# The opening of a gated block kernel: first loads, the split of x, and TensorE before its inputs

## The reference

```python
proj = rmsnorm(x, gla_norm) @ gla_w_in        # 2048 x 6160
q, k, v, r, g_low = split(proj)               # k is computed first
...                                           # gated linear attention, output product
h = h + squared_relu_mlp(rmsnorm(h))          # 2048 -> 8192 -> 2048
h = rmsnorm(h, final_norm)
...                                           # second block: stick-breaking attention beside
                                              # a recurrent unit, input and output products
```

## Time and profile before

| what | value |
|---|---|
| median of 3 runs | 1518.81 us (1517.96 to 1520.08) |
| span of the profiled execution, first to last instruction | 1514.3 us |
| TensorE busy in that span | 1497.6 us |
| mean granted TensorE clock in that span | 1.000 |

### The profile page before, as it was taken

How to read it: one execution, slowest core, us unless ns; L and a number is a source line. 1 busy time by engine, 2 the same in 40 slices (tenths; PEclk the granted TensorE clock), 3 DMA queues, 4 the chain that set the end, 5 groups by cost and what they waited for, 6 DMA issues and landing times. The chain is left out here.

```text
span 1514.3 us, 19184 instructions
## 1 busy us (share of the span) xinstructions
PE 1497.6 (99%) x6826; PEld 1237.1 (82%) x6826; DVE 843.5 (56%) x872; ACT 711.9 (47%) x856; POOL 30.8 (2%) x54
## 2 busy tenths in 40 slices
PE   7999999999999999999999999999999999999998
PEld 6788888888888888888888888888888888888886
DVE  5555545555555545555555554555566776565653
ACT  5544544445444433443344433444654664565532
POOL 3000000000000000000000000000000011000000
PEclk9999999999999999999999999999999999999999
DMA  8455565657666666666666666666556566545564
GB/s 267 137 167 154 145 202 176 187 176 240 192 183 182 192 192 194 185 182 188 194 189 184 189 190 191 189 190 185 182 180 181 154 194 191 166 144 167 181 193 140
DMA packets 144721, 277.03 MB, mean 183 GB/s; under 512 B 10800, under 2 KB 10912, under 8 KB 144512
## 3 DMA queue, kind: packets, MB, share of 16 engines
q1 hardware_dynamic: 143056, 271.75, 59.3%
q0 software_dynamic: 1040, 3.07, 0.6%
q10 hardware_dynamic: 544, 1.05, 0.2%
HBM read 273.74 MB, written 2.10 MB: 182 GB/s over the span
## 5 line engine op out<-in xcount | busy, mean ns | idle before, releaser
L1003 DVE TENSOR_TENSOR w_lo<-raw,w_hi 128x1024 fp32r<-128x1024 f32 x508 | 620.2, 1225 | 610.7 <-ACT w_hi L706 609.3
L706 ACT ACTIVATE w_hi<-raw 128x1024 fp32r<-128x1024 f32 x508 | 537.0, 1059 | 731.7 <-PE acc L420 710.5
L418 PE MATMUL acc<-w_hi,xa_hi 128*128 128x512 f32 x1276 | 506.3, 397 | 1.6 <-issue 1.4
L420 PE MATMUL acc<-w_hi,xa_lo 128*128 128x512 f32 x1276 | 497.3, 390 | 0.0
L419 PE MATMUL acc<-w_lo,xa_hi 128*128 128x512 f32 x1276 | 496.7, 389 | 0.0
L418 PE MATMUL acc<-w_hi,xb_hi 128*128 128x512 f32 x768 | 300.1, 391 | 1.5 <-DVE w_lo L1003 1.5
L420 PE MATMUL acc<-w_hi,xb_lo 128*128 128x512 f32 x768 | 299.0, 389 | 0.0
L419 PE MATMUL acc<-w_lo,xb_hi 128*128 128x512 f32 x768 | 298.8, 389 | 0.0
L418 PEld LDWEIGHTS acc<-w_hi,xa_hi 128*128 128x128 f32 x1276 | 239.7, 188 | 52.0 <-issue 3.2
L420 PEld LDWEIGHTS acc<-w_hi,xa_lo 128*128 128x128 f32 x1276 | 239.5, 188 | 50.7
L419 PEld LDWEIGHTS acc<-w_lo,xa_hi 128*128 128x128 f32 x1276 | 239.9, 188 | 49.4 <-issue 1.9
(11 more groups left out here) (198 smaller groups left out, 513.1 us busy)
## 6 DMA issues: line engine op xcount, KB each, us to landing
raw<-in_mlp_w_up SPq DMA_DIRECT2D x128, 512.0 KB, 3.7
raw<-in_mlp_w_down SPq DMA_DIRECT2D x128, 512.0 KB, 4.4
raw<-in_gla_w_in SPq DMA_DIRECT2D x96, 512.0 KB, 3.8
raw<-in_w_in SPq DMA_DIRECT2D x96, 512.0 KB, 3.7
raw<-in_gla_w_out SPq DMA_DIRECT2D x32, 512.0 KB, 4.5
raw<-in_w_out SPq DMA_DIRECT2D x32, 512.0 KB, 4.7
result<-stage SPq DMA_DIRECT2D x8, 256.0 KB, 3.3
h<-in_x ACTq DMA_DIRECT2D x2, 512.0 KB, 6.4
```

Source lines behind the costliest of these rows:

```text
L418: pe.matmul(o, xh[:, kt, xs], w_hi[:, n % RING, k, :], start=kt == 0, stop=False)
L420: last = pe.matmul(o, xl[:, kt, xs], w_hi[:, n % RING, k, :], start=False, stop=kt == KT - 1)
L706: act.activation(w_hi[:, n % RING, :, :], raw[:, n % RING, :, :], ACT.Copy)\
L1003: dve.tensor_tensor(w_lo[:, n % RING, :, :], raw[:, n % RING, :, :], w_hi[:, n % RING, :, :].bitcast(F32), ALU.subtract).then_inc(lo_ready, 1)
```

## The change

The first loads are cut and ordered anew. The order in SP's queue becomes: `gla_norm`, chunk 0 in two halves of 256 KB, chunk 1, x columns 512 to 1023, chunk 2, x columns 1024 to 1535, chunk 3, x columns 1536 to 2047, `wg_raw`, then chunks 4 to 7. ScalarE's queue loads x columns 0 to 255 and 256 to 511 (256 KB each, with a semaphore for each). ScalarE splits group 0 of x ahead of chunk 0, and chunk 0 in two halves, each with a signal; VectorE makes `xa_lo` of group 0 ahead of `w_lo` of chunk 0. TensorE starts the first two matmuls of chunk 0 when the first half is there. `turn_x(c + 2)` now follows chunk c for c from 0 to 5. Around the first turns TensorE does 16 transposes of `ident` by `ident` whose result nobody reads.

```diff
@@ SP
-            for c in range(RING):
+            for k, done in ((0, first_in), (1, raw_in[0])):
+                sp.dma_start(raw[:, 0, k, :], w_in_v[:, k, GH * GDK:GH * GDK + N]).then_inc(done, 16)
+            for c in range(1, CH):
                 load(c, 0, None, CH, w_in_v[:, CK * c:CK * c + CK, GH * GDK:GH * GDK + N])
-
-            for j in (2, 3):
-                sp.dma_start(h[:, :, j * N:(j + 1) * N], x_v[:, :, j * N:(j + 1) * N])\
-                    .then_inc(x_in[j], 16)
-            sp.dma_start(wg_raw, w_in_v[:, :, 2 * GH * GDK + 2 * D:]).then_inc(wg_in, 16)
-            for c in range(RING, CH):
-                load(c, 0, None, CH, w_in_v[:, CK * c:CK * c + CK, GH * GDK:GH * GDK + N])
+                if c <= 3:
+                    sp.dma_start(h[:, :, c * N:(c + 1) * N], x_v[:, :, c * N:(c + 1) * N])\
+                        .then_inc(x_in[c + 1], 16)
+                if c == 3:
+                    sp.dma_start(wg_raw, w_in_v[:, :, 2 * GH * GDK + 2 * D:]).then_inc(wg_in, 16)
@@ TensorE, multiply_first
-                pe.wait_ge(hi_ready, 1)
+                pe.wait_ge(first_hi, 1)
...
+                        if kt == 1 and ws is w_hi and xs is xa_hi:
+                            pe.wait_ge(hi_ready, 1)
@@ TensorE, turn_x
-                if g % 2 == 0:
-                    pe.wait_ge(x_in[g // 2], 16)
+                if g < 2 or g % 2 == 0:
+                    pe.wait_ge(x_in[g if g < 2 else g // 2 + 1], 16)
@@ TensorE, after
-                    if c == 0:
-                        turn_x(2)
-                        turn_x(3)
-                    if 1 <= c <= 4:
-                        turn_x(c + 3)
+                    if c <= 5:
+                        turn_x(c + 2)
@@ TensorE, start
+            def keep_running(n):
+
+                for _ in range(n):
+                    pe.transpose(aux[:, 0, 0:P], ident[:, :], ident[:, :])
+
             pe.wait_ge(pool_chain, 2)
+            keep_running(6)
             pe.wait_ge(norm_in, 16)
             pe.transpose(aux[:, 1, 0:KT], rows[0:KT, :], ident[0:KT, 0:KT]).then_inc(par_turned, 1)
+            keep_running(5)
             turn_x(0)
             turn_x(1)
+            keep_running(5)
@@ ScalarE, start
-                act.dma_start(h[:, :, j * N:(j + 1) * N], x_v[:, :, j * N:(j + 1) * N])\
+                act.dma_start(h[:, :, j * S:(j + 1) * S], x_v[:, :, j * S:(j + 1) * S])\
                     .then_inc(x_in[j], 16)
 
-            act.wait_ge(raw_in[0], 16)
-            act.activation(w_hi[:, 0, :, :], raw[:, 0, :, :], ACT.Copy).then_inc(hi_ready, 1)
             act.wait_ge(par_ready, 1)
             split_x(None, 0, xa_hi, 0, C_GLA, 1)
+            for k, arrived, done in ((0, first_in, first_hi), (1, raw_in[0], hi_ready)):
+                act.wait_ge(arrived, 16)
+                act.activation(w_hi[:, 0, k, :], raw[:, 0, k, :], ACT.Copy).then_inc(done, 1)
@@ VectorE, start
             for n in range(RING):
-                if n:
-                    rest_x(n % 2, xa_hi, xa_lo, 2 * n, C_GLA, n + 1)
+                rest_x(n % 2, xa_hi, xa_lo, 2 * n, C_GLA, n + 1)
...
-                if n == 0:
-                    rest_x(0, xa_hi, xa_lo, 0, C_GLA, 1)
```

More of the change, by code:

```diff
@@ L197, in gated_block_kernel @@
         par_in, par_turned, par_ready = sem("par_in"), sem("par_turned"), sem("par_ready")
-        x_in = [sem(f"x_in{i}") for i in range(4)]
+        x_in = [sem(f"x_in{i}") for i in range(5)]
+        first_in, first_hi = sem("first_in"), sem("first_hi")
         gain_in, up_in, wg_in = sem("gain_in"), sem("up_in"), sem("wg_in")
```

## The result

| | before | after |
|---|---|---|
| median of 21 runs each, side by side | 1517.28 us | 1520.11 us |
| lowest to highest | 1514.63 to 1520.08 | 1518.12 to 1522.78 |
| span of the profiled execution | 1514.3 us | 1518.2 us |

The ratio is 1.0017, with a 95% interval from 1.0011 to 1.0023. The kernel is some 2.8 us slower by the medians, 2.7 by the means. That is under the 0.2% that the prediction called a change that can be told, but 21 runs tell it from none. The point forecast was no change.

The account below looks back on a forecast made before the run. The loads were taken to bound the kernel up to 26.5 us, TensorE after. The 2.4 to 4.1 us won at chunk 0 were all given back: span 1514.2 plus 4.5 gives 1518.7 us, range 1517.0 to 1521.3.

Parts of the forecast that it names:

- what paces the opening: Up to 26.5 us the loads set the pace, chunk 4 hanging on chunk 5's landing at 23.25; TensorE itself after it.
- The chunk 0 win: TensorE starts chunk 0 at 7.7 us instead of 10.14 and ends it 2.4 to 4.1 us earlier.
- Clock lost in the wait: Rival: TensorE's clock falls in the wait before chunk 4, costing 2.4 us and up to a microsecond more; 1521.1 us; chance 0.2.
- the fast start: TensorE runs chunk 0 at full clock from the start, chunk 3 ending at about 21.3 us; given half.
- a wait over 3.5 us: Condition for the clock to fall before chunk 4, read from 3.5 us of idleness ahead of a fall at the span's end.
- The wait of 2.8 to 5.1 us: TensorE's forecast idle time right before chunk 4, where it waited 1.0 us before the change.
- the likeliest case: The point forecast: the chunk 0 win is all given back at chunk 4, time 1518.7 us; chance 0.6.
- The bytes ahead of chunk 5 stay the same, as do POOL's: Loads: as POOL's instructions are untouched, chunk 4 still lands at about 21.9 us and chunk 5 at 23.25.
- thin pieces: Rival: x rows of 1 KB slow the loads, chunk 5 lands up to 1.0 us later, 1519.2 to 1519.7; chance 0.1.
- the forecast's 26.4: Start of chunk 4 on TensorE once group 4's xa_lo is ready, instead of 26.9 us before.
- the forecast's 35.7: Start of the gate matmuls on TensorE, from 32.93 + 2.74 us.
- The rule on transposes: By the skill, transposes do not count as clock activity; then the idle turns are for nothing and the start is slow.

Follow-up runs that it names:

- e3: The 16 turns of ident alone added to the kernel before; 1517.96 us, ratio 0.9998.
- e4: The new order of turns alone (group c + 2 behind chunk c) put into the kernel before; 1517.58 us, ratio 0.9998.
- e12: Kernel after plus x split two chunks sooner, 128x7 matmuls cut, o_gain held, ScalarE's table loaded up front, 14 ident turns behind chunk 3; 1518.62 us, ratio 1.0012.
- e14: Kernel after plus x split two chunks sooner, 128x7 matmuls cut, o_gain held, ScalarE's table loaded up front, no added ident turns; 1515.14 us, ratio 0.9987.
- e2: Kernel after without its 16 turns of ident; 1518.18 us, ratio 1.0005 to the kernel before.
- e13: Kernel after with POOL's load of o_gain started early, right behind that of b_gate; 1518.63 us, ratio 1.0013 to the kernel before.
- e8: Only the new loads of SP and ScalarE, with their semaphores, put into the kernel before; 1518.42 us, ratio 1.0009.
- e9: Kernel after with POOL's load of o_gain held until w_lo of chunk 8 is written; 1517.18 us, ratio 1.0000 to the kernel before.
- e1: Kernel after with 36 more turns of ident filling TensorE's wait ahead of chunk 4; 1517.40 us, ratio 0.9999 to the kernel before.
- e10: Kernel after with the wait ahead of chunk 4 filled by 36 ident turns and the 128x7 matmuls cut in halves; 1516.03 us, ratio 0.9995.
- e5: Kernel after with groups 4 to 7 of x split two chunks sooner by ScalarE and VectorE; 1517.31 us, ratio 1.0000 to the kernel before.
- e7: Kernel before with the 32 matmuls of 128x7 cut in two halves, two chunks apart; 1515.94 us, ratio 0.9991.

## Why the prediction was wrong, point by point

*Right: what paces the opening.* The loads set the pace up to chunk 4, through `w_hi`, `w_lo` and `xa_lo` of group 4. The chunk 0 win was 3.0 us, inside 2.4 to 4.1, and all was given back: forecast and found. e3 and e4 (0.9998 each) confirm that the idle turns and the order of turns are worth nothing by themselves. Chunk 0 started at 8.56, not 7.7. TensorE had no wait there; it was still at its turns, because columns 256 to 511 of x landed at 6.7, where before all 512 were there at 5.5:

```profile
6.70 1.11 PE L450 MATMUL tp<-ident,h 128*128 128x128 f32 x4 [0.93 <-DMA h<-in_x]
```

ScalarE's table load (1.28 us) also moved, from 1.8 us, where ScalarE had nothing to do, to 5.86, behind its wait for the first turn (ScalarE's rows above). It is not what set the start: e12 and e14 load the table at 0.81 and start chunk 0 at 8.62 and 9.25. The miss was free, since TensorE had to wait ahead of chunk 4 anyway.

*Wrong: the weight and the condition of the rival "Clock lost in the wait".* This rival is what happened, at its price: forecast 2.4 us and up to one more, found 2.7 in the trace. It was given a chance of 0.2 by two steps. The first, that it needs the fast start and a wait over 3.5 us, rested on one fall at the end of the span. e2 (2.48 us) and e13 (2.90) speak against the length, e2 and e8 (3.63), both without turns of `ident`, against the need of a fast start. The wait of 2.8 to 5.1 us that the forecast itself wrote down lies where such falls were seen (2.48 to 5.14 us, with 3.05 in e9 as the exception). The second step was to leave the likeliest case at full clock with such a wait in it.

*Mis-sized: "The bytes ahead of chunk 5 stay the same, as do POOL's".* The bytes did, their order did not. The 1.5 us of later landing are the late `o_gain` (e9, e13). The step took an untouched instruction list for an untouched timeline. As all of the wait sits ahead of chunk 4, it goes one to one into the end: 27.90 against the forecast's 26.4.

*Right: thin pieces do not delay chunk 5.* The row 8.56 to 12.30 has 386 GB/s, and e13 and e8, which have the same pieces, get chunk 5 at 23.29 and 23.36. The second piece of x itself did come late, at 6.7, and at 6.3 to 7.4 in the other traces with the new loads, against 5.4 to 5.5 with the old; whether by its size or by the order, no run tells. In the prediction's argument the 381 GB/s "on a single queue" are a misreading: that is all queues together, and SP's alone moved 2.31 MB in those 7.5 us, 308 GB/s.

*The sum again.* In the trace the gate matmuls are 4.3 us behind the forecast's 35.7: 1.5 landing, 2.8 clock. Over the runs it is less, since before also loses clock in some. After spends 7.9 - 4.7 = 3.2 us more at half clock, of which half is lost, 1.6 us; the rest of the 2.7, some 1.1, may be the landing. That split is worked out, not isolated. e1 and e9 each aim at one of the two and each gives back all, with a mean clock that won only 1.1 and 0.9 us (0.9981 and 0.9980 against 0.9974). So the clock's part is shown, by e8 without a late landing and by e10 with the clock held; how the rest divides between the landing and other things stays open.

*The number.* 1520.1 against a forecast of 1518.7 looks closer than it was. The 1518.7 stood on three runs of before with a median of 1518.81, and 21 runs give 1517.28. No change would have been 1517.2, so the miss is 2.9 us, not 1.4. The 4.5 us that the prediction put between span and time hold that luck too: in after's profiled execution the two, 1518.2 and 1520.3, lie 2.1 us apart.

*The rule on transposes.* In the prediction, the Trainium skill ("TensorE: Matmul & The Clock Gate", Part 4) had idle turns count for nothing. The clock rose here when only turns had run. TensorE's timeline in e10, with the same turns as after:

```profile
4.70 1.06 PE L450 MATMUL tp<-ident,h 128*128 128x128 f32 x4
6.38 0.66 PE L450 MATMUL tp<-ident,h 128*128 128x128 f32 x4 [0.62 <-DMA h<-in_x]
6.87 0.71 PE L678 MATMUL aux<-ident 128*128 128x128 f32 x5
8.55 1.25 PE L438 MATMUL acc<-w_hi,xa_hi 128*128 128x512 f32 x4 [0.97 <-ACT w_hi L987]
```

Four turns cost 1.06 us, the next four 0.66; chunk 0 then starts fast (four matmuls in 1.25 us, against 2.04 in the earlier trace rows). That rule does not hold here, and the measurement decides. The fill of e1 and e10, 36 such turns, fits that. The early rise was so in two traces, e5 and e10; in the other seven with these turns the rise came inside chunk 0. From its first matmul to the turn behind it, chunk 0 takes 4.1 us on average over nine traces with the turns and 4.7 over the eight without. The turns bring about 0.6 us there, where it is hidden.

## What to carry to other kernels

Work won ahead of a transfer that gates a later step only lengthens the wait there, and on TensorE the clock can fall on top: here a wait of 2.5 us was enough. Before reordering loads, take away the dependency that makes the wait (here 8 small splits moved two chunks earlier), or fill it. And an engine whose code is untouched can still be moved in time by its neighbour: check each queue's start times, not its instruction list.

## What the runs showed that I had not expected

- The clock fell 0.8 us after work had resumed in e2, following a 2.48 us hole, while a hole of 3.05 us in e9 left it up.
- A TensorE that is busy without a gap can lose its clock: 3.63 us of matmuls with seven columns each went ahead of a fall in five of the eleven traces that have them in one piece. In the six traces that have two halves of 1.84 us there is no such fall, and the clock over the runs of e7 rose to 0.9996.
- POOL's small instructions took up to 1.32 us instead of 0.29 while VectorE made `w_lo` (0.93 in e13, 0.87 once in before). That the one causes the other is not isolated.
- TensorE's issue waits at the MLP loop went from 0.6 to 5.6 us with 14 transposes added 590 us earlier.
